# Feed-forward products of 512 moving columns where two streams, or two halves of one input, meet the same weights

## The chip, the cores and the metric

One NeuronCore of a Trainium2 chip. The metric is the device time of one launch in microseconds; three runs of the kernel before took 2554.95 us (median), 2552.15 and 2566.07 us.

## The reference

Two blocks of depth 2, all in fp32, for 256 tokens of width 1024. The first block is a mixer (convolution, attention, gated linear attention) with a feed-forward part on `x`. The second block works on two inputs, the image `x` (256 tokens) and a context (256 tokens), with the same weights for both. For each of its layers it does

- `swiglu_half_step(x, ...)` and the same on the context, with `w_ffn_up[l, 0]` and `w_ffn_down[l, 0]`;
- a modulated norm, projections, attention over both inputs and an output projection;
- `swiglu_half_step` again with the second pair of weights; in the last layer for the image alone.

`swiglu_half_step` is `x + 0.5 * mod[j+2] * ((silu(gt) * up) @ w_down)` with `gt, up = split(h @ w_up)` and `h = modulate(rms_norm(x))`; the inner width is 2816, that is 11 pairs of 256. `mod` comes from `silu(cond) @ w_ada`, for 144 weight tiles in all.

## The kernel before

**Weights.** All weights come as a stream of 510 units of 128x1024 fp32 (512 KB each). SP loads a unit into `W_raw` (`load`, L770) when the unit six places earlier is finished; ACT copies it rounded to fp32r as `W_hi` (`split`, L1448); DVE subtracts to get `W_lo` (`split`, L1825). A product of fp32 accuracy is then three fp32r products, `W_lo*x_hi`, `W_hi*x_lo` and `W_hi*x_hi` (`three`, L926 to L930). A unit is 8 weight tiles of 128x128, so it takes 24 matmuls, each with its own weight load and 256 moving columns, for one stream. PE takes unit g when `W_lo` for it is there (`weights`, L921); splits are issued three units ahead.

**Streams.** The image is stream A, the context stream B. `make_streams` lists for each the stages (norm, ffn, in2, att2, out2) and their steps; a step is a weight unit or a piece of other work. `make_order` (L305) weaves both lists by rules into one order, `ORDER`, which all engines follow: A takes a shared unit first, B takes it two or three steps later (`LAG`), and it is final when B is done. So in a feed-forward stage (66 units: 44 for up, 22 for down, in groups of six and five pairs) PE alternates 24 matmuls for A and 24 for B. PSUM is two slots of two banks for each stream (`ps`, L660), used in turn.

**Elementwise work.** After the four up units of a pair ACT takes the silu of the gate half (L1554) and DVE multiplies it with the other half out of PSUM (L2049), ACT rounds the result (L1561) and DVE takes the rest (L2055). After the down units of a group DVE adds `gate * result` to `X` (`update`, L1897; `finish_update`, L1904, for a stage's last part, which is issued in the norm of the next stage). A norm squares `X`, sums on DVE (L1917) and on PE (`norm_sums`, L1008, 1-column matmuls L1014), spreads the root on PE (L1002) and writes `H_hi` and `H_lo` (L1960).

**Conditioning.** `place_ada` (L374) gives each of 144 tiles `A_raw` a step: two DVE instructions of 1024 elements each (`ada`, L1833, L1842), loaded by SP (L778). In the second block every final unit of a feed-forward stage gets one until they are used up.

The stages that the change touches are the three joint feed-forward stages (layer 0 before and after the attention, layer 1 before it) and the image's last one, where only stream A is left.

## Time and profile before

| what | value |
|---|---|
| median of 3 runs | 2554.95 us (2552.15 to 2566.07) |
| profiled execution | span 2549.3 us; its own time is not given apart from that, and the span is 5.65 us under the median |
| PE matmul / weight load busy | 2391.4 us (94%) / 2322.8 us (91%), 20452 of each |
| DVE / ACT / POOL busy | 1661.0 us (65%) / 997.7 us (39%) / 188.2 us (7%) |
| mean granted TensorE clock | 0.966 |
| DMA | 352.78 MB, mean 138 GB/s |

A matmul's record is longer than the distance to the next one (0.28 us against about 0.12 us), since they are pipelined: the pace is read from start to start. PEld is the weight load of a matmul; a window's columns are its span, then busy us and instruction count of each engine, the granted clock of PE, the busy share of the DMA engines and GB/s.

### The profile page before, as it was taken

How to read it: one execution, taken by the hardware profiler on the slowest of the kernel's cores; microseconds unless marked ns; L12 is line 12 of the kernel's file. 1: busy time of each engine (PE TensorE's matmuls, PEld its weight loads, DVE VectorE, ACT ScalarE, POOL GpSimd, SP SyncE). 2: the span in 40 equal slices, each digit the busy share in tenths (PEclk: the TensorE clock that was granted, in tenths of full speed). 3: DMA queues.
4: the chain of work that ended last, by engine and by line, in shares of the span. 5: the costliest groups of instructions: out<-in, count | busy, mean ns of one | idle time of the engine just before them, and what ended most of it. 6: DMA issues, size and time to landing. Idle time of an engine off the chain costs nothing. (4 is left out here: it accounts for less than half of the span.)

```text
span 2549.3 us, 47682 instructions
## 1 busy us (share of the span) xinstructions
PE 2391.4 (94%) x20452; PEld 2322.8 (91%) x20452; DVE 1661.0 (65%) x2777; ACT 997.7 (39%) x1468; POOL 188.2 (7%) x300
## 2 busy tenths in 40 slices
PE   7989998899799999999788999998999998988999
PEld 7889997899799999899558999998999998967999
DVE  6789888788877777744775677776333336376554
ACT  6455664465432222322473222223222223145543
POOL 0000000370000000011000900000000000100000
PEclk9899998999899999999898999999999999999999
DMA  6246652456445555412001455552222222211454
GB/s 256 95 157 226 221 190 92 144 197 237 141 143 191 188 182 187 169 59 79 14 1 67 164 190 189 186 198 91 92 96 96 100 100 96 70 52 67 162 194 157
DMA packets 104306, 352.78 MB, mean 138 GB/s; under 512 B 18976, under 2 KB 19232, under 8 KB 103840
## 3 DMA queue, kind: packets, MB, share of 16 engines
q1 hardware_dynamic: 95904, 348.94, 38.9%
q8 instruction: 161, 2.64, 0.4%
q0 software_dynamic: 8192, 0.80, 0.3%
q14 instruction: 49, 0.40, 0.1%
HBM read 348.63 MB, written 1.05 MB: 137 GB/s over the span
## 5 line engine op out<-in xcount | busy, mean ns | idle before, releaser
L1456 ACT ACTIVATE W_hi<-W_raw 128x1024 fp32r<-128x1024 f32 x510 | 538.7, 1060 | 1119.6 <-PE slot L930 1053.9
L1830 DVE TENSOR_TENSOR W_lo<-W_raw,W_hi 128x1024 fp32r<-128x1024 f32 x510 | 621.5, 1222 | 473.8 <-ACT W_hi L1456 465.1
L928 PE MATMUL slot<-H_hiA,W_lo 128*128 128x256 f32 x2768 | 790.9, 286 | 18.0 <-DVE H_loA L1960 4.6
L929 PE MATMUL slot<-H_loA,W_hi 128*128 128x256 f32 x2768 | 781.5, 282 | 0.0
L930 PE MATMUL slot<-H_hiA,W_hi 128*128 128x256 f32 x2768 | 780.9, 282 | 0.0
L928 PEld LDWEIGHTS slot<-H_hiA,W_lo 128*128 128x128 f32 x2768 | 533.3, 193 | 29.5 <-issue 21.1
L929 PEld LDWEIGHTS slot<-H_loA,W_hi 128*128 128x128 f32 x2768 | 535.8, 194 | 0.1
L930 PEld LDWEIGHTS slot<-H_hiA,W_hi 128*128 128x128 f32 x2768 | 532.7, 192 | 0.0
L1842 DVE SCALAR_TENSOR_TENSOR PROD<-A_raw,SC 128x1024 bf16<-128x1024 f32 x288 | 341.2, 1222 | 170.3 <-DMA A_raw<-adastream 169.8
L928 PE MATMUL slot<-H_hiB,W_lo 128*128 128x256 f32 x1376 | 385.9, 280 | 3.0 <-DVE VB L2347 1.3
L929 PE MATMUL slot<-H_loB,W_hi 128*128 128x256 f32 x1376 | 383.9, 279 | 0.0
L930 PE MATMUL slot<-H_hiB,W_hi 128*128 128x256 f32 x1376 | 383.9, 279 | 0.0
L928 PE MATMUL slot<-HIDA,W_lo 128*128 128x256 f32 x1056 | 293.6, 278 | 1.2 <-DVE HIDA L2055 1.2
L929 PE MATMUL slot<-HIDA,W_hi 128*128 128x256 f32 x1056 | 293.5, 278 | 0.0
L930 PE MATMUL slot<-HIDA,W_hi 128*128 128x256 f32 x1056 | 293.5, 278 | 0.0
L928 PEld LDWEIGHTS slot<-H_hiB,W_lo 128*128 128x128 f32 x1376 | 259.2, 188 | 4.6 <-issue 2.2
L929 PEld LDWEIGHTS slot<-H_loB,W_hi 128*128 128x128 f32 x1376 | 260.7, 189 | 0.0
L930 PEld LDWEIGHTS slot<-H_hiB,W_hi 128*128 128x128 f32 x1376 | 259.7, 189 | 0.0
L928 PEld LDWEIGHTS slot<-HIDA,W_lo 128*128 128x128 f32 x1056 | 198.2, 188 | 1.6 <-DVE W_lo L1830 1.0
L929 PEld LDWEIGHTS slot<-HIDA,W_hi 128*128 128x128 f32 x1056 | 199.5, 189 | 0.0
L930 PEld LDWEIGHTS slot<-HIDA,W_hi 128*128 128x128 f32 x1056 | 198.6, 188 | 0.0
L820 POOL TENSOR_TENSOR R0A<-V_A,EXPO 128x2 f32<-128x2 f32 (+3 forms) x25 | 38.7, 1549 | 2005.2 <-DVE V_A L1868 2005.2
(277 smaller groups left out, 3057.8 us busy)
## 6 DMA issues: line engine op xcount, KB each, us to landing
W_raw<-wstream SPq DMA_DIRECT2D x510, 512.0 KB, 3.3
A_raw<-adastream SPq DMA_DIRECT2D x144, 512.0 KB, 4.3
BT<-par POOLq DMA_DIRECT2D x256, 3.0 KB, 2.6
XA<-xT SPq DMA_DIRECT2D x2, 512.0 KB, 4.5
SC<-cond SPq DMA_DIRECT2D x1, 1024.0 KB, 14.4
XB<-ctxT SPq DMA_DIRECT2D x1, 1024.0 KB, 16.4
CON<-const SPq DMA_DIRECT2D x1, 960.5 KB, 9.6
PAR<-par SPq DMA_DIRECT2D x1, 680.0 KB, 10.8
```

The costliest lines, as they stand in the source:

```text
L820: pool.tensor_tensor(s.R0[:, 0:n], s.V_[:, 0:n], EXPO[:, 0:n], ALU.pow).then_inc(s.sem.r0, 1)
L928: pe.matmul(out, wl, xh, start=start, stop=False, skip_group_check=True)
L929: pe.matmul(out, wh, xl, start=False, stop=False, skip_group_check=True)
L930: return pe.matmul(out, wh, xh, start=False, stop=stop, skip_group_check=True)
L1456: act.activation(W_hi[:, g % HIGH, :], W_raw[:, g % RAW, :], ACT.Copy).then_inc(S.w_hi, 1)
L1830: dve.tensor_tensor(W_lo[:, g % RAW, :], W_raw[:, g % RAW, :], W_hi[:, g % HIGH, :].bitcast(F32), ALU.subtract).then_inc(S.w_lo, 1)
L1842: a = dve.scalar_tensor_tensor(PROD[:, b, :], A_raw[:, slot, :], 1.0, SC[:, b, :], ALU.mult, ALU.mult, accum_out=MOD[:, t // MODS, t % MOD ...
```

## The change

Three kinds of stage take the place of `ffn` in the second block. `ffnj` (stream A) and `ffnb` (stream B) are a joint stage. Of its 66 units the first three (`LEAD`) and the last five (`TAIL`) are still done for A and for B in 24 matmuls each; the other 58 are done once, in 24 matmuls of 512 moving columns, the 256 of A and the 256 of B (`joined`). Their input tiles `HJ` and `HIDJ` are the old ones under one name, so the moving operand is two runs of 256 columns, and the result fills a PSUM bank. A unit of both streams uses four banks, half of PSUM, the halves in turn (`shared`). Silu, product, rounding and rest are one instruction for both streams. `ffns` is the image's last stage: a weight tile's `W_lo*x_hi` is a product of 256 columns, and `W_hi` meets `x_hi` and `x_lo` in one of 512, whose two results lie in two halves of a bank; ACT copies the second half out (`CORR`) and DVE adds it, or DVE adds both to `X` in turn. Its last five units are done in three products as before. The steps of `ffnb` and so the shared units are eight; the order rules are unchanged. The conditioning tiles are spread evenly over the 58 joint units of each joint stage: 48, 24 and 48 tiles in place of 62, 58 and none.

```diff
+LEAD = 3
+TAIL = GROUPS[-1][1] - GROUPS[-1][0]
...
+        if blk == 2 and not solo:
+            stages[s][-1].place = 1 if s == "A" else None
+            if s == "A":
+                st = add(s, "ffnj", steps, solo, dict(tok=PAIRS + 2 * len(GROUPS), pair=PAIRS), l=l, blk=blk, ffn=which)
+                both[l, which] = st
+                old = Old(s, 2, tok, (l, 2 * which), st.side, 0, tok)
+            else:
+                mate = both[l, which]
+                st = add(s, "ffnb", steps[:LEAD] + steps[-TAIL:], solo, dict(tok=1), l=l, blk=blk, ffn=which, mate=mate)
+                mate.mate = st
+                old = Old(s, 2, st.tok, (l, 2 * which), mate.side, 1, mate.tok + PAIRS + 2 * len(GROUPS) - 1)
+            stages[s][-1].end = old
+            side[s] = 1 - side[s]
+            return old
+        if blk == 2:
+            before = stages[s][-1]
+            side[s] = 1 - before.tok % 4 // 2
+            add(s, "ffns", steps, solo, dict(tok=PAIRS + 2 * len(GROUPS), pair=PAIRS), l=l, blk=blk, ffn=which)
+            stages[s][-1].end = Old(s, 2, tok, (l, 2 * which), side[s], 0)
+            return stages[s][-1].end
...
+    shares = {(0, 0): 2 * 3 * KT, (0, 1): 3 * KT, (1, 0): 2 * 3 * KT}
+    free = {k: [v for v in ORDER if v.stage.kind == "ffnj" and (v.stage.l, v.stage.ffn) == k and v.final] for k in shares}
+    for k, n in shares.items():
+        for i, v in enumerate(free[k]):
+            v.ada = (i + 1) * n // len(free[k]) - i * n // len(free[k])
...
-        elif st.kind == "ffn" and st.blk == 2:
-            v.ada = int(left > 4)
...
+        HJ = at("HJ", 40 * K + 192, [P, 2, 2, KT, SEQ], F32R)
+        HIDJ = at("HIDJ", AA, [P, 2, (AB - AA) // 4], F32R)
+        HFJ = at("HFJ", AA, [P, 2, (AB - AA) // 4])
...
-        slots = [ctx.enter_context(nc.psum_tensor(f"slot{i}", [P, 2, 512], F32)) for i in range(4)]
+        banks = ctx.enter_context(nc.psum_tensor("banks", [P, 8, 512], F32))
+        slots = [banks[:, 2 * i:2 * i + 2, :] for i in range(4)]
 
         def ps(st, tok):
             if st.ring == 4:
                 return slots[tok % 4]
-            return slots[tok % 2 + (2 if st.s == "B" else 0)]
+            return slots[2 * st.side + (tok % 2 if st.place is None else st.place)]
+        def shared(st, n):
+            h = 4 * ((st.side + n) % 2)
+            return banks[:, h:h + 4, :]
...
+                if st.old is not None and st.old.both is not None:
+                    pe.wait_ge(A.sem.evac, st.old.both + (s is B))
+                if st.place is not None:
+                    wait(pe, s.sem.evac, norm_token(st))
...
+            def joined(out, wl, wh, lo, hi, start, stop):
+                out = out.rearrange("p (s n) -> p s n", s=2)
+                pe.matmul(out, wl, hi, start=start, stop=False, skip_group_check=True)
+                pe.matmul(out, wh, lo, start=False, stop=False, skip_group_check=True)
+                return pe.matmul(out, wh, hi, start=False, stop=stop, skip_group_check=True)
+            def up_part(s, st, q, first):
+                wl, wh = weights()
+                p = shared(st, 0)
+                hw = s.sem.h_ready
+                h0 = (st if s is A else st.mate).hr - 8
+                for t in range(2):
+                    for k in range(4):
+                        kt = 4 * (q % 2) + k
+                        if t == 0 and q < 2:
+                            pe.wait_ge(hw, h0 + kt + 1)
+                        c = slice(256 * k + P * t, 256 * k + P * t + P)
+                        mm = three(p[:, 2 * (q // 2) + t, SEQ * s.half:SEQ * s.half + SEQ], wl[:, c], wh[:, c],
+                                   s.H_lo[:, kt, :], s.H_hi[:, kt, :], s is A and kt == 0, False)
+                mm.then_inc(s.sem.done, 1)
+            def up_both(st, n, q):
+                wl, wh = weights()
+                p = shared(st, n)
+                for t in range(2):
+                    for k in range(4):
+                        kt = 4 * (q % 2) + k
+                        c = slice(256 * k + P * t, 256 * k + P * t + P)
+                        mm = joined(p[:, 2 * (q // 2) + t, :], wl[:, c], wh[:, c], HJ[:, :, 1, kt, :],
+                                    HJ[:, :, 0, kt, :], kt == 0, kt == 7)
+                mm.then_inc(A.sem.done, 1)
+            def hidden(j, low, k):
+                o = 2 * SEQ * (2 * j + low) + SEQ * k
+                return HIDJ[:, :, o:o + SEQ]
+            def down_both(st, n, j, first, last):
+                wl, wh = weights()
+                p = shared(st, n)
+                for k in range(2):
+                    for t in range(4):
+                        c = slice(512 * k + P * t, 512 * k + P * t + P)
+                        mm = joined(p[:, t, :], wl[:, c], wh[:, c], hidden(j, 1, k), hidden(j, 0, k),
+                                    first and k == 0, last and k == 1)
+                mm.then_inc(A.sem.done, 1)
+            def down_part(s, st, old, j, first, last):
+                wl, wh = weights()
+                out = blocks(old, old.tok)
+                for k in range(2):
+                    for t in range(4):
+                        c = slice(512 * k + P * t, 512 * k + P * t + P)
+                        x = slice(SEQ * k, SEQ * k + SEQ)
+                        mm = three(out[:, t, :], wl[:, c], wh[:, c], s.HID[:, j, 1, x], s.HID[:, j, 0, x],
+                                   first and k == 0 and t % 2 == 0, last and k == 1)
+                mm.then_inc(s.sem.done, 1)
+            def doubled(bank, wl, wh, pair, start, stop):
+                pe.matmul(bank[:, 0:SEQ], wl, pair[:, 0, :], start=start, stop=False, skip_group_check=True)
+                return pe.matmul(bank.rearrange("p (s n) -> p s n", s=2), wh, pair, start=False, stop=stop,
+                                 skip_group_check=True)
+            def ffns(s, st):
+                n = 0
+                for a, b in GROUPS:
+                    for m in range(a, b):
+                        wait(pe, s.sem.evac, st.tok + n - 1)
+                        p = shared(st, n)
+                        for q in range(4):
+                            wl, wh = weights()
+                            for t in range(2):
+                                for k in range(4):
+                                    kt = 4 * (q % 2) + k
+                                    if n == 0 and t == 0 and q < 2:
+                                        pe.wait_ge(s.sem.h_ready, st.hr - 8 + kt + 1)
+                                    c = slice(256 * k + P * t, 256 * k + P * t + P)
+                                    mm = doubled(p[:, 2 * (q // 2) + t, :], wl[:, c], wh[:, c], HJ[:, s.half, :, kt, :],
+                                                 kt == 0, kt == 7)
+                            mm.then_inc(s.sem.done, 1)
+                            yield
+                        n += 1
+                    for half in range(2):
+                        pe.wait_ge(s.sem.evac, st.tok + n - 1)
+                        p = shared(st, n)
+                        for j in range(a, b):
+                            pe.wait_ge(s.sem.hid_ready, st.pair + j + 1)
+                            if b == PAIRS and half:
+                                down_part(s, st, st.end, j - a, j == a, j == b - 1)
+                                yield
+                                continue
+                            wl, wh = weights()
+                            for k in range(2):
+                                for t in range(4):
+                                    c = slice(512 * k + P * t, 512 * k + P * t + P)
+                                    x = slice(SEQ * k, SEQ * k + SEQ)
+                                    mm = doubled(p[:, t, :], wl[:, c], wh[:, c], s.HID[:, j - a, :, x],
+                                                 j == a and k == 0, j == b - 1 and k == 1)
+                            mm.then_inc(s.sem.done, 1)
+                            yield
+                        n += 1
...
+            def ffnj(s, st):
+                for q in range(LEAD):
+                    if q == 2:
+                        pe.wait_ge(A.sem.evac, st.tok)
+                    up_part(A, st, q, q == 0)
+                    yield
+                n, i = 0, LEAD
+                for a, b in GROUPS:
+                    for m in range(a, b):
+                        if n == 1:
+                            pe.wait_ge(B.sem.evac, st.mate.tok)
+                        if n:
+                            pe.wait_ge(A.sem.evac, st.tok + n - 1)
+                        for q in range(LEAD if n == 0 else 0, 4):
+                            up_both(st, n, q)
+                            i += 1
+                            yield
+                        n += 1
+                    for half in range(2):
+                        pe.wait_ge(A.sem.evac, st.tok + n - 1)
+                        for j in range(a, b):
+                            pe.wait_ge(A.sem.hid_ready, st.pair + j + 1)
+                            if i < len(st.steps) - TAIL:
+                                down_both(st, n, j - a, j == a, j == b - 1)
+                            else:
+                                down_part(A, st, st.end, j - a, j == a, j == b - 1)
+                            i += 1
+                            yield
+                        n += 1
+            def ffnb(s, st):
+                for q in range(LEAD):
+                    up_part(B, st.mate, q, False)
+                    yield
+                for j in range(TAIL):
+                    down_part(B, st, st.end, j, j == 0, j == TAIL - 1)
+                    yield
...
+            def ffns(s, st):
...
+                            if j == 0:
+                                act.wait_ge(s.sem.done, v + 4 * m + 4)
+                                wait(act, s.sem.hid_f32, pair)
+                                act.activation(CORR[:, :, :], shared(st, a + m + 2 * i)[:, :, SEQ:2 * SEQ], ACT.Copy)\
+                                   .then_inc(S.corr_out, 1)
+                                act.wait_ge(S.gate_sum, a + m + 1)
+                                act.activation(SGJ[:, 1, :], SGJ[:, 0, :], ACT.Silu).then_inc(s.sem.silued, 1)
...
+            def ffnj(s, st):
...
+                                act.activation(SGJ[:, :, :], shared(st, a + m + 2 * i)[:, 0:2, :], ACT.Silu)\
+                                   .then_inc(s.sem.silued, 1)
...
+            def update_both(st, gate, n, m, done):
+                dve.wait_ge(A.sem.done, done)
+                dve.wait_ge(A.sem.evac, st.tok + n)
+                p = shared(st, n)
+                for s in (A, B):
+                    b = p[:, :, SEQ * s.half:SEQ * s.half + SEQ]
+                    update_half(s, b, gate, m, 0)
+                    a = update_half(s, b, gate, m, 1)
+                a.then_inc(A.sem.evac, 1)
...
+            def ffns(s, st):
...
+                            if j == 0:
+                                dve.wait_ge(S.corr_out, a + m + 1)
+                                wait(dve, s.sem.silued, pair)
+                                dve.tensor_tensor(gates[:, 0, :, :], p[:, 0:2, 0:SEQ], CORR[:, 0:2, :], ALU.add)\
+                                   .then_inc(S.gate_sum, 1)
+                                step(dve.tensor_tensor(out, p[:, 2:4, 0:SEQ], CORR[:, 2:4, :], ALU.add))
+                                release(S.gate_sum, a + m + 1, s.sem.evac, st.tok + first + m)
...
+            def ffnj(s, st):
...
+                            if j == 1:
+                                dve.wait_ge(s.sem.silued, pair + 1)
+                                p = shared(st, first + m)
+                                split3 = lambda x: x.rearrange("p t (s n) -> p t s n", s=2)
+                                out = HFJ[:, :, o + 2 * SEQ:o + 4 * SEQ].rearrange("p s (t n) -> p t s n", t=2)
+                                dve.tensor_tensor(out, split3(SGJ[:, :, :]), split3(p[:, 2:4, :]), ALU.mult)\
+                                   .then_inc(s.sem.hid_f32, 1)
+                                release(s.sem.hid_f32, pair + 1, s.sem.evac, st.tok + first + m)
+                            if j == 2:
+                                dve.wait_ge(s.sem.hid_hi, pair + 1)
+                                dve.tensor_tensor(HIDJ[:, :, o + 2 * SEQ:o + 4 * SEQ], HFJ[:, :, o + 2 * SEQ:o + 4 * SEQ],
+                                                  HIDJ[:, :, o:o + 2 * SEQ].bitcast(F32), ALU.subtract)\
+                                   .then_inc(s.sem.hid_ready, 1)
...
```

## Rows read from the trace of the kernel before

**Rows 1.** The page: span, and busy time of PE and its weight loads.

```profile
span 2549.3 us, 47682 instructions
...
PE 2391.4 (94%) x20452; PEld 2322.8 (91%) x20452; DVE 1661.0 (65%) x2777; ACT 997.7 (39%) x1468; POOL 188.2 (7%) x300
```

**Rows 2.** Windows: the three joint feed-forward stages, then the image's last one.

```profile
705.00:1087.00 382.00, 373.67 (x3159) 373.23 (x3157) 276.49 (x434) 103.83 (x126) 1.39 (x2) 0.99 0.49 177
1405.00:1775.00 370.00, 363.66 (x3126) 362.94 (x3124) 263.23 (x411) 102.64 (x123) 57.20 (x120) 0.99 0.49 175
1788.00:2152.00 364.00, 355.51 (x3121) 355.08 (x3120) 130.12 (x174) 101.51 (x124) 1.40 (x2) 0.99 0.28 96
2362.00:2549.30 187.30, 182.45 (x1584) 182.12 (x1584) 101.97 (x115) 82.36 (x93) 0.00 (x0) 0.98 0.50 175
```

**Rows 3.** Windows of 50 us inside the first and the third joint stage.

```profile
750.00:800.00 50.00, 50.00 (x427) 50.00 (x426) 37.80 (x55) 14.71 (x19) 0.00 (x0) 1.00 0.51 183
1800.00:1850.00 50.00, 50.00 (x444) 50.00 (x443) 16.42 (x18) 14.31 (x18) 0.00 (x0) 1.00 0.28 96
```

**Rows 4.** Timeline of PE from 900 us, first and last of 19 (start us, us, what).

```profile
899.82 0.28 PE L928 MATMUL slot<-H_hiA,W_lo 128*128 128x256 f32 x1
...
901.94 0.28 PE L928 MATMUL slot<-HIDB,W_lo 128*128 128x256 f32 x1
```

**Rows 5.** Timeline of PE, the step at 1600 us.

```profile
1600.19 0.28 PE L930 MATMUL slot<-HIDB,W_hi 128*128 128x256 f32 x1
1600.45 0.39 PE L928 MATMUL slot<-H_hiA,W_lo 128*128 128x256 f32 x1
```

**Rows 6.** Timeline of PE from 1612 us, first and last of 20.

```profile
1611.80 0.28 PE L928 MATMUL slot<-H_hiA,W_lo 128*128 128x256 f32 x1
...
1613.95 0.28 PE L929 MATMUL slot<-H_loA,W_hi 128*128 128x256 f32 x1
```

**Rows 7.** Timeline of PE: fp32 products of 256 columns, one row for four.

```profile
123.17 1.02 PE L1275 MATMUL slot<-AC,CON 128*128 128x256 f32 x4
```

**Rows 8.** That line alone: shortest, median and longest ns.

```profile
L1275 PE MATMUL slot<-AC,CON x8: 377/378/379, 123.2 to 454.8; 128*128 128x256 f32 x8
```

**Rows 9.** Timeline of PE: 1-column products at full clock.

```profile
1068.60 1.47 PE L1014 MATMUL slot<-CON,SQA 128*128 128x1 f32 x12
```

**Rows 10.** That line alone for stream A: shortest, median, longest ns.

```profile
L1014 PE MATMUL slot<-CON,SQA x132: 164/250/353, 9.0 to 2358.0; 128*128 128x1 f32 x132
```

**Rows 11.** Timeline of PE: the same at half clock, and the first products after.

```profile
1082.01 2.69 PE L1014 MATMUL slot<-CON,SQB 128*128 128x1 f32 x12 [5.96 <-DVE SQB L1917]
1087.05 0.69 PE L1002 MATMUL slot<-CON,RSB 128*128 128x128 f32 x2 [2.35 <-DVE RSB L1874]
...
1087.75 0.42 PE L929 MATMUL slot<-H_loA,W_hi 128*128 128x256 f32 x1
1087.97 0.41 PE L930 MATMUL slot<-H_hiA,W_hi 128*128 128x256 f32 x1
```

**Rows 12.** Lines: fp32 products whose weights have 16 rows.

```profile
L1150 PE MATMUL slot<-GG,PAR x8: 374/374/478, 37.6 to 365.7; 16*128 16x256 f32 x8
```

**Rows 13.** Lines of DVE in the first joint stage (count, busy us, mean ns, idle before).

```profile
L1842 DVE SCALAR_TENSOR_TENSOR PROD<-A_raw,SC 128x1024 bf16<-128x1024 f32 x124 | 147.0, 1223 | 88.8 <-DMA A_raw<-adastream 88.5 <-DVEq L1881 0.2
L1830 DVE TENSOR_TENSOR W_lo<-W_raw,W_hi 128x1024 fp32r<-128x1024 f32 x66 | 80.6, 1220 | 13.7 <-ACT W_hi L1456 11.8 <-DVEq L1881 1.9
...
L2049 DVE TENSOR_TENSOR HFA<-SGA,slot 128x512 f32<-128x512 f32 x11 | 7.5, 683 | 0.0
...
L1892 DVE SCALAR_TENSOR_TENSOR XA<-slot,GATE,XA 128x256 f32<-128x256 f32 x16 | 6.6, 476 | 0.5 <-PE slot L930 0.5
```

**Rows 14.** Lines of ACT in the first joint stage.

```profile
L1456 ACT ACTIVATE W_hi<-W_raw 128x1024 fp32r<-128x1024 f32 x66 | 70.0, 1061 | 239.2 <-PE slot L930 239.2
...
L1554 ACT ACTIVATE SGA<-slot 128x512 f32<-128x512 f32 x11 | 6.6, 600 | 18.8 <-PE slot L930 18.8
```

**Rows 15.** Windows: where DMA moved the most.

```profile
550.00:600.00 50.00, 50.00 (x427) 50.00 (x427) 45.67 (x63) 22.71 (x25) 5.33 (x12) 1.00 0.74 259
```

145 lines of the change are left out of this document (121 added, 24 removed).

## The prediction

> **What bounds the kernel now.** I start from the page: PE is busy for 94% of the span and its weight loads for 91%, nobody else is above 65% [rows 1]. Next the windows over the stages that the change touches [rows 2]: in the three joint feed-forward stages (382, 370 and 364 us) PE is busy for 98% at a granted clock of 0.99, and in the image's last stage for 182 of 187 us. So here time is PE time, and what counts is the distance from one matmul to the next. The windows of 50 us [rows 3] show PE without any idle time in them, yet with 427 matmuls in the first stage and 444 in the third, at the same granted clock of 1.00 (2.4 GHz). The timeline gives the two paces: 18 distances between 899.82 and 901.94 us, 117.8 ns each [rows 4], and 19 between 1611.80 and 1613.95, 113.2 ns each [rows 6] (I use 113.3, of which 443 to 444 fit in 50 us). The first holds for the whole first stage and in the second up to 1600 us, where one product comes 0.26 us after its forerunner [rows 5]; afterwards the pace is the quicker one, and stays so to the end of the third stage.
>
> 256 columns alone need less. At half clock fp32r products of 256 columns follow each other in about 0.22 us [rows 11], so at full clock they would need about 107 ns. What holds them up is seen where the columns are few: 12 products of one column with a full weight load take 1.47 us, the last of them 0.25, so 111 ns each [rows 9, 10], and at half clock (2.69 - 0.35) / 11 = 213 ns [rows 10, 11]. A pair of weight load and product thus costs the load's 111 ns whatever its columns, up to about 256, and with 256 both sides are so near each other that 113.3 or 117.8 come out.
>
> **What the change does to PE.** Of the 66 units of a joint stage 58 are done in 24 products of 512 columns in place of 48 of 256. Per stage that makes 58 * 24 = 1392 pairs of products joined. Where were they? In the first stage all 1392 at 117.8 ns; in the second 33 units (36 of the first group less the three leading ones), 792 pairs, at 117.8, and 25 units, 600 pairs, at 113.3; in the third 1392 at 113.3. So 2184 pairs cost 2 * 117.8 = 235.6 ns and 1992 cost 226.6 ns.
>
> What does a product of 512 columns cost? The trace has none. Its bounds: below, twice the columns at full clock with the load wholly hidden, 213 ns (256 columns at half clock are the same number of 1.2 GHz cycles) [rows 11]; above, two old products, 226.6. The nearest row is the fp32 product of line 1275, whose four records take 1.02 us with the last 0.377 long, so 214 ns each [rows 7], and whose record is 378 ns long where that of 256 fp32r columns is 280 [rows 6, 8]; 98 ns more than the 113 to 118 of the old pace is 211 to 216. It occupies the array twice as long as an fp32r one, with a full weight load beside it, and that load doesn't show. I take 215 ns, the upper part of what these rows allow.
>
> Joint stages: 2184 * (235.6 - 215) = 45.0 us and 1992 * (226.6 - 215) = 23.1 us, together **68.1 us**.
>
> The image's last stage: 61 of its 66 units change, 8 tiles each, 488 triples. A triple was 3 * 113.3 = 340 ns. Now it is a product of 256 columns followed by one of 512. The load of the long product has to run beside the short one, so that one stays at 113.3; the other load hides. 113.3 + 215 = 328.3, so 11.7 * 488 = **5.7 us**.
>
> The Trainium skill ("TensorE: Matmul & The Clock Gate", section "Back-to-back issue gap") states a distance of N/2.4 + 2.5 ns for a warm stream; by it a pair of 256 costs 218.4, one product of 512 costs 215.8, and all that could be won in the joint stages would be about 11 us. The rows here contradict it at 256 columns.
>
> **What else changes, and what hides it.**
> - Silu, product, rounding and rest for both streams are one instruction of twice the size instead of two: ACT's 600 ns and DVE's 683 ns become about twice that at most, so no more in sum [rows 13, 14]. The result is due after a whole further pair (four units of 24 * 215 = 5.2 us), and `hid_ready` of a group's last pair is waited for four units or more after its up units.
> - `update_both` is eight times 0.41 us (16 of them are busy for 6.6 us [rows 13]) = 3.3 us in one go. It stands before the splits of two later units. Three units of weights are split ahead, 15 us; a full DVE step (1.2 for the split, 2.4 for a conditioning tile, 3.3) is 6.9 us. Hidden; without that cover 3.3 us for each of ten or so places.
> - Conditioning tiles move from the first two stages to the third. There DVE is busy for 130 of 364 us [rows 2] and gets 48 * 2.45 = 118 us more, DMA goes from 96 GB/s to under 190, which the first stage bears already. Nothing on the path; in the first stage DVE gets relief that PE doesn't feel. SP's loads of weights stand before its conditioning loads in each step, and those two queues carried the same mix before.
> - The last stage gets a copy of 1024 elements (ACT, 1.06 us by the nearest row [rows 14]) and two additions of 512 (0.68 us each [rows 13]) for a pair, four updates more for a half. In four units of 2.63 us ACT needs 4.2 + 1.1 + 0.6 + 0.6 and waits 0.7 for DVE's sum: 7.2 of 10.5 us. DVE needs 4.9 + 1.4 + 1.4. Weights are called for at 512 KB in 2.63 us, 200 GB/s; 259 were moved elsewhere [rows 15].
> - New waits on PE: A's norm waits for all earlier tokens of A. Its sums wait for squares of the same updates anyway, so the wait ends earlier than the one behind it. The wait of the third leading unit and of the second pair are for norm tokens freed when `H_lo` was done. Behind B's norm the order is the same: PE idles 5.96 us for B's squares and 2.35 us for its root at half clock before and after the change [rows 11]. B's three leading units now stand together, and the joint units wait for both; before, A had one unit in between. `H_lo` of B is complete before A's three leading units are, so nothing comes late. 0 us, at most one B unit of 2.8 us in each of three places.
>
> **Sum.** 68.1 + 5.7 = 73.8 us. The profiled span of 2549.3 becomes 2475.5; the median of the runs lies 5.65 us above the span, so 2554.95 - 73.8 = **2481 us**.
>
> **The rivals.**
> *Excess for each product.* Of the 113.3 or 117.8 ns, 6.6 or 11.1 belong to every product whatever its width. Then 512 columns cost 220 or 224.4 ns; 2184 * 11.2 + 1992 * 6.6 + 488 * 6.7 = 41 us, 2514 us. For it: two paces with no visible cause, neither of which is the load's 111. Against: line 1275 shows 214. The skill's rule above is the same mechanism with a smaller excess, and would give 2543.
> *No gain from width.* The hardware takes the two runs of 256 columns as two products, each at the old pace: 2549 to 2555 us. Against: the weight loads are halved in any case, and they set the pace.
> *The load no longer hides.* The slower side. The products of line 1150, with weights of 16 rows, have some records of 478 ns among those of 374 [rows 12]: 104 ns more, a load that stands alone. If a load waited so for the end of every long product, it would cost 320 ns in place of 231.3 (the mean of the old pairs, which is the point that decides), 4176 * 88.7 = 370 us, 2925 us. Against: with 128 rows the loads run beside their products in every row shown.
> A smaller doubt: products that stay at 256 columns run at either pace, and the gap that switches it [rows 5] may fall elsewhere. A window outside the joint stages has the slow pace too, 427 in 50 us [rows 15]; as an estimate, three such stretches, 1300 products at 4.5 ns, are 6 us either way.
>
> **How the numbers follow.** Forecast 0.77; excess for each product 0.15; no gain 0.04; load not hidden 0.04. The range: below, 213 instead of 215 ns (9 us) and 6 us of pace, 2466; above, up to the second case, 2515. That leaves out 8% of rivals and the edges of the first two. Half a per cent (12.8 us) is about what a measurement of this kernel can tell from no change. Both leading cases are faster by more: 0.92; within 0.5% 0.04; slower 0.04.
>
> **What would show it.** In the profile after: matmuls of 128x512 with starts 215 ns apart, in stretches of either old pace; 58 units of about 5.2 us, joint stages of some 353, 347 and 348 us; matmuls fewer by 4176 + 488; in the last stage triples of 328 ns. The paces of the 256-column products next to them tell whether the switch moved. Wrong it would be by distances of 220 or more, by PE idle before `W_lo` or `HIDJ`, or by a longer wait for B's squares than 5.96 us.

## The result, and the profile after

The changed kernel takes **2578.80 us** (median of 9 runs, 2572.84 to 2583.67) against 2555.91 us (9 runs, 2545.60 to 2573.63) of the kernel before: ratio 1.0095, 95% interval 1.0064 to 1.0125. It is slower by about 1%, where 2481 us was forecast. The profiled executions have spans of 2571.0 and 2549.3 us, so 21.7 us are to be explained. Runs more than 1.5% above the fastest of their kernel stand in the ranges given here, but not in the ratios.

The page of the changed kernel, the lines that answer to [rows 1], and one of its groups of matmuls:

```profile
span 2571.0 us, 38123 instructions
PE 2411.0 (94%) x15788; PEld 2129.8 (83%) x15788; DVE 1674.2 (65%) x2745; ACT 996.1 (39%) x1413; POOL 188.4 (7%) x300
L1130 PE MATMUL banks<-HJ,W_hi 128*128 128x512 f32 x984 | 389.2, 396 | 0.0
```

The matmuls are fewer by 20452 - 15788 = 4664 = 4176 + 488, so the change does all that it says. Weight loads were busy for 91% of the span and are now for 83%: they have been relieved, and PE has not become quicker. A product of 512 columns has a record of 396 ns, where the fp32 product from which I had priced it has 378 [rows 8]. Windows of 50 us in the first and the third joint stage (as [rows 3]) and in the image's last stage:

```profile
750.00:800.00 50.00, 50.00 (x216) 40.30 (x215) 33.16 (x45) 14.19 (x14) 0.00 (x0) 1.00 0.50 169
1800.00:1850.00 50.00, 50.00 (x216) 40.26 (x215) 30.33 (x38) 12.88 (x14) 0.00 (x0) 1.00 0.44 148
2400.00:2450.00 50.00, 50.00 (x285) 43.42 (x284) 31.39 (x35) 27.78 (x31) 0.00 (x0) 1.00 0.60 184
```

PE has no idle time and the clock is granted in full, as before. But 216 products of 512 fit where 427 or 444 of 256 did. A window also counts the one or two products that overlap its edges, so the distance is taken from the timeline of PE, between the first and last start of a stretch. Here 26 distances in the first joint stage, and then nine triples of the last stage:

```profile
899.77 0.40 PE L1130 MATMUL banks<-HIDJ,W_hi 128*128 128x512 f32 x1
900.01 0.39 PE L1131 MATMUL banks<-HIDJ,W_hi 128*128 128x512 f32 x1
900.24 0.40 PE L1129 MATMUL banks<-HIDJ,W_lo 128*128 128x512 f32 x1
...
905.84 0.40 PE L1129 MATMUL banks<-HIDJ,W_lo 128*128 128x512 f32 x1
```

```profile
2399.76 0.28 PE L1190 MATMUL banks<-HJ,W_lo 128*128 128x256 f32 x1
2399.88 0.40 PE L1191 MATMUL banks<-HJ,W_hi 128*128 128x512 f32 x1
2400.12 0.28 PE L1190 MATMUL banks<-HJ,W_lo 128*128 128x256 f32 x1
...
2402.95 0.28 PE L1190 MATMUL banks<-HJ,W_lo 128*128 128x256 f32 x1
```

(905.84 - 899.77) / 26 = 233.5 ns; over many such stretches it is **233.3 ns**, in all three joint stages, whatever the pace of the products of 256 around them. It is a mean of two values: in the trace's nanoseconds 236.0 and 230.7 take turns (213 distances from 750 to 800 us), and as they go by twos and the products of a weight tile by threes, each of the three products has one value and then the other. A triple costs (2402.95 - 2399.76) / 9 = 354 ns (353.3 over more of them), the short product 118 of it and the long one 235. Forecast were 215 and 328.3.

Did a wait come in? The sums of the squares in front of each norm are landmarks that both kernels have. The timeline of PE of the changed kernel has them here, five times B's and then A's of the last stage, from the second on with the idle time before it:

```profile
692.85 0.35 PE L1064 MATMUL banks<-CON,SQB 128*128 128x1 f32 x1
1081.97 0.34 PE L1064 MATMUL banks<-CON,SQB 128*128 128x1 f32 x1 [6.04 <-DVE SQB L2169]
1391.67 0.34 PE L1064 MATMUL banks<-CON,SQB 128*128 128x1 f32 x1 [7.53 <-DVE SQB L2169]
1775.00 0.34 PE L1064 MATMUL banks<-CON,SQB 128*128 128x1 f32 x1 [5.96 <-DVE SQB L2169]
2159.38 0.34 PE L1064 MATMUL banks<-CON,SQB 128*128 128x1 f32 x1 [6.04 <-DVE SQB L2169]
2370.48 0.34 PE L1064 MATMUL banks<-CON,SQA 128*128 128x1 f32 x1 [4.13 <-DVE SQA L2169]
```

and the kernel before has the first and the last four of them here:

```profile
688.82 0.35 PE L1014 MATMUL slot<-CON,SQB 128*128 128x1 f32 x1
1389.97 0.34 PE L1014 MATMUL slot<-CON,SQB 128*128 128x1 f32 x1 [7.60 <-DVE SQB L1917]
1772.58 0.34 PE L1014 MATMUL slot<-CON,SQB 128*128 128x1 f32 x1 [5.96 <-DVE SQB L1917]
2146.70 0.34 PE L1014 MATMUL slot<-CON,SQB 128*128 128x1 f32 x1 [5.96 <-DVE SQB L1917]
2355.68 0.34 PE L1014 MATMUL slot<-CON,SQA 128*128 128x1 f32 x1 [4.24 <-DVE SQA L1917]
```

The idle times are the old ones within 0.1 us (the one left out stands in [rows 11] with 5.96 at 1082.01). The differences of the landmarks give the time by stage: +4.0 us in front of the first joint stage, -0.04 at its end, +1.7 after the attention behind it, +2.4 after the second joint stage, **+12.7 after the third**, +14.8 at the start of the last stage, **+21.7** at the end. So within the stages that the change touches the loss lies in the third joint stage (10.3 us) and in the last one (6.9 us), and these are the stretches in which the kernel before had its quick pace. The distances account for it: 2184 pairs that had cost 235.6 ns cost 2.3 ns less, -5 us; 1992 pairs that had cost 226.6 cost 6.7 more, +13.3 us; 488 triples cost 353.3 instead of 340, +6.5 us. That makes 14.8 us. By stage it is -3.2, +2.2 and +9.3 for the joint stages, where the landmarks give -4.1, +0.7 and +10.3. The other 7.9 us lie outside these stages: 4.0 before the first joint one (692.85 against 688.82 us) and 3.9 in the two attention parts, where nothing is joined. In the first of these stretches it is the clock: PE has half clock for 78 us of it, where the kernel before has 65 (the mean over the whole execution is 0.961 and was 0.966). As an estimate, those 13 us more cost up to 6.5 us, and 613 fewer distances at 117.8 ns give 2.7 back, so up to 3.8 of the 4.0 us. In the third joint stage 3.4 us more at half clock are up to 1.7 us.

**Theory W (width):** an fp32r column has its own price, above 1/2.4 ns, whatever the width; the weight load was never the limit. **Rivals:** L, the weight load still sets the distance; R, the jump between the two runs of 256 in the moving operand does; K, consecutive writes to one bank do; P, each product has 20 ns on top of its columns, whatever its width. (The expectations call W theory C or B, and K theory S.) The question beside them is why 256 columns cost 113.3 at one time and 117.8 at another.

### The profile page after: what moved, and what is told of

It is laid out like the page before. It is cut to its first block and busy times, and to the rows that moved or that the text cites. A ratio compares the mean times of both kernels' runs of the same rounds, so it can differ in the third digit from the quotient of the medians.

```text
span 2571.0 us, 38123 instructions
## 1 busy us (share of the span) xinstructions
PE 2411.0 (94%) x15788; PEld 2129.8 (83%) x15788; DVE 1674.2 (65%) x2745; ACT 996.1 (39%) x1413; POOL 188.4 (7%) x300
## 5 line engine op out<-in xcount | busy, mean ns | idle before, releaser
L974 PE MATMUL banks<-HJ,W_lo 128*128 128x256 f32 x1824 | 528.7, 290 | 19.2 <-DVE HJ L2209 4.4
L975 PE MATMUL banks<-HJ,W_hi 128*128 128x256 f32 x1824 | 518.3, 284 | 0.0
L976 PE MATMUL banks<-HJ,W_hi 128*128 128x256 f32 x1824 | 517.7, 284 | 0.0
L1130 PE MATMUL banks<-HJ,W_hi 128*128 128x512 f32 x984 | 389.2, 396 | 0.0
L1131 PE MATMUL banks<-HJ,W_hi 128*128 128x512 f32 x984 | 389.2, 396 | 0.0
L1129 PE MATMUL banks<-HJ,W_lo 128*128 128x512 f32 x984 | 389.2, 395 | 0.0
L974 PEld LDWEIGHTS banks<-HJ,W_lo 128*128 128x128 f32 x1824 | 356.2, 195 | 30.9 <-issue 20.7
L975 PEld LDWEIGHTS banks<-HJ,W_hi 128*128 128x128 f32 x1824 | 355.9, 195 | 0.1
L976 PEld LDWEIGHTS banks<-HJ,W_hi 128*128 128x128 f32 x1824 | 354.8, 195 | 0.0
L1131 PEld LDWEIGHTS banks<-HJ,W_hi 128*128 128x128 f32 x984 | 185.0, 188 | 44.6
L1129 PEld LDWEIGHTS banks<-HJ,W_lo 128*128 128x128 f32 x984 | 185.0, 188 | 44.5
L1130 PEld LDWEIGHTS banks<-HJ,W_hi 128*128 128x128 f32 x984 | 185.0, 188 | 44.4
L974 PE MATMUL banks<-HIDJ,W_lo 128*128 128x256 f32 x632 | 176.3, 279 | 1.8 <-DVE HIDJ L2307 1.7
L975 PE MATMUL banks<-HIDJ,W_hi 128*128 128x256 f32 x632 | 175.4, 278 | 0.0
L976 PE MATMUL banks<-HIDJ,W_hi 128*128 128x256 f32 x632 | 175.4, 278 | 0.0
L1129 PE MATMUL banks<-HIDJ,W_lo 128*128 128x512 f32 x408 | 161.4, 396 | 0.0
L1130 PE MATMUL banks<-HIDJ,W_hi 128*128 128x512 f32 x408 | 161.4, 396 | 0.0
L1131 PE MATMUL banks<-HIDJ,W_hi 128*128 128x512 f32 x408 | 161.4, 396 | 0.0
```

The costliest lines, as they stand in the source:

```text
L974: pe.matmul(out, wl, xh, start=start, stop=False, skip_group_check=True)
L975: pe.matmul(out, wh, xl, start=False, stop=False, skip_group_check=True)
L976: return pe.matmul(out, wh, xh, start=False, stop=stop, skip_group_check=True)
L1129: pe.matmul(out, wl, hi, start=start, stop=False, skip_group_check=True)
L1130: pe.matmul(out, wh, lo, start=False, stop=False, skip_group_check=True)
L1131: return pe.matmul(out, wh, hi, start=False, stop=stop, skip_group_check=True)
```

## Experiments

The probes p1, p2, p5, p7 and p8 change only what the joint products multiply, each of the three joint stages in its own way (stages 0-0, 0-1 and 1-0 of the code). What they compute there is another thing than the reference; the order of instructions, waits and loads is that of the changed kernel. Their total times therefore say nothing, their distances do. All edits are shown shortened. Expectations call the kernels' stages "first", "second" and "third".

### p1: one run, 384 columns, narrow weights

```diff
+ if key == (0, 0): hi, lo = one_run[0], one_run[1]      # 512 columns in one run of HJ
+ if key == (0, 1): out, hi, lo = out[:, :, 0:192], hi[:, :, 0:192], lo[:, :, 0:192]
+ if key == (1, 0): out, wl, wh = out[0:64], wl[:, 0:64], wh[:, 0:64]
```

> Three probes in one kernel, one for each joint stage; results are not the reference's. First stage: the moving operand of every 512-column product is one run of 512 columns (two neighbouring tiles of stream A) in place of two runs of 256. Second stage: 2 runs of 192, so 384 columns. Third stage: 512 columns, but weights of 64 columns, so half a load and 64 output rows. Theory R (the switch between two runs costs the time): first stage 215 ns a product, second 160 + 18 = 178, third 233. Theory C (at full clock fp32r columns enter at 233.3 / 512 = 0.456 ns each): 233, 175, 233. Theory L (the weight load beside the product takes turns from it): 233, 180, 223. Theory P (an excess of 20 ns for each product whatever its size): 233, 180, 233; at 384 columns C and P are 5 ns apart.

Measured, by windows inside the three stages:

```profile
850.00:900.00 50.00, 50.00 (x216) 40.30 (x215) 33.34 (x54) 10.50 (x10) 0.00 (x0) 1.00 0.48 169
1450.00:1500.00 50.00, 50.00 (x290) 50.00 (x290) 32.96 (x39) 18.41 (x19) 8.85 (x19) 1.00 0.55 180
1850.00:1900.00 50.00, 50.00 (x216) 29.07 (x215) 32.48 (x54) 9.55 (x9) 0.00 (x0) 1.00 0.49 168
```

One run of 512 columns is as slow as two (216; start to start 233.3 ns), which ends R. With weights of 64 columns the loads are busy for 29.07 us in place of 40.30 and the products come 0.6 ns sooner (216; 232.7 ns), which ends L for 512 columns. 384 columns cost 173.3 ns (36 distances in 6.24 us), 13.3 above 384/2.4, where P had 180.

### p2: bf16, two banks in turn, 320 columns

```diff
+ if key == (0, 0): wl = wh = HALF[:, 0:P]; hi = lo = HALF[:, P:P + 512]   # bf16 ones
+ if key == (0, 1): outs = [pair[n], pair[1 - n], pair[n]]                 # banks in turn
+ if key == (1, 0): outs, hi, lo = [out[:, :, 0:160]] * 3, hi[:, :, 0:160], lo[:, :, 0:160]
```

> Three probes in one kernel; results are not the reference's. First stage: both operands of the 512-column products are bf16 (one constant tile, 512 columns in one run). Second stage: consecutive products write to different PSUM banks in turn. Third stage: 2 runs of 160, so 320 columns. Theory C with bytes as its reason (fp32r operands come in slower than the array takes them at full clock): 213 to 216 ns, 233, 146. Theory S (adding to the bank that was just written costs it): 233 (fp32 results are added there too), 213 to 216, 146 to 153. Theory R (two runs): 215, 233, 133 + 18 = 151. Theory P (fixed excess of 20 ns): 233, 233, 153.

The timeline of PE in the first stage, first and last of 15, and the window of the second:

```profile
900.80 0.38 PE L1143 MATMUL banks<-HALF 128*128 128x512 bf16 x1
...
903.82 0.38 PE L1142 MATMUL banks<-HALF 128*128 128x512 bf16 x1
1450.00:1500.00 50.00, 50.00 (x216) 40.30 (x215) 23.25 (x27) 13.47 (x14) 0.00 (x0) 1.00 0.41 135
```

bf16 needs 3.02 / 14 = 215.7 ns. The Trainium skill ("TensorE: Matmul & The Clock Gate", "Back-to-back issue gap") has N/2.4 + 2.5 ns, 215.8 for 512: this probe agrees with it, so the rule that I had set aside holds, here for bf16 only. The section calls it the gap of an isolated product, and gives about 131 ns for 512 columns in a stream of loads and products; no run here shows that. Two banks in turn change nothing (216; 233.3 ns), which ends K. 320 columns take 146.7 ns (42 distances in 6.16 us), as W expected.

### p5: constants in fp32r, 448 and 480 columns

```diff
+ if key == (0, 0): wl = wh = CONST[:, 0:P]; hi = lo = CONST[:, P:P + 512]   # fp32r ones, one run
+ if key == (0, 1): out, hi, lo = out[:, :, 0:224], hi[:, :, 0:224], lo[:, :, 0:224]
+ if key == (1, 0): out, hi, lo = out[:, :, 0:240], hi[:, :, 0:240], lo[:, :, 0:240]
```

> Three probes in one kernel; results are not the reference's. So far 256 columns cost 6.7 or 11.1 ns over their columns at 2.4 GHz, 320 and 384 cost 13.3, 512 cost 20.0, and 512 bf16 columns 2.3. First stage: the control to the bf16 probe, both operands fp32r from one constant tile of ones, 512 columns in one run. Second stage: 2 runs of 224, 448 columns; third: 2 runs of 240, 480 columns. Theory B (four-byte columns are what cannot come in at 2.4 GHz without stalls, whatever they hold): 233 ns; and stalls of 6.7 ns, one more for every 170 to 190 columns: 448 columns 186.7 + 13.3 to 20 = 200 to 207, 480 columns 220. Theory A (the address changes or the data, not the width of a column, cost it): the constant tile gives 216.

The timeline of the first stage, first and last of 28, then the windows of the second and third:

```profile
899.78 0.39 PE L1140 MATMUL banks<-CONST 128*128 128x512 f32 x1
...
905.90 0.39 PE L1140 MATMUL banks<-CONST 128*128 128x512 f32 x1
1500.00:1550.00 50.00, 50.00 (x249) 46.31 (x248) 28.26 (x40) 13.27 (x13) 0.00 (x0) 1.00 0.44 148
1900.00:1950.00 50.00, 50.00 (x236) 44.07 (x235) 35.71 (x52) 11.46 (x12) 0.00 (x0) 1.00 0.54 188
```

With constants 512 fp32r columns take 6.12 / 27 = 226.7 ns, that is 2 * 113.3: **a column costs in the quick pace of the kernel before what it costs in a product of 512 from constants**, 0.443 ns. Neither 233 nor 216, the two expectations, came out. 448 columns take 202.7, 480 take 213.3 where 220 was expected. All widths together, with the excess over N/2.4:

| columns | 256 | 320 | 384 | 448 | 480 | 512 | 512, constants | 512, bf16 |
|---|---|---|---|---|---|---|---|---|
| ns | 113.3 / 117.8 | 146.7 | 173.3 | 202.7 | 213.3 | 233.3 | 226.7 | 215.7 |
| excess | 6.7 / 11.1 | 13.3 | 13.3 | 16.0 | 13.3 | 20.0 | 13.3 | 2.4 |

No width between is cheaper per column than 256 at its quick pace.

### p7: which of the two operands

```diff
+ if key == (0, 0): wl = wh = CONST[:, 0:P]              # constant weights, real moving columns
+ if key == (0, 1): hi = lo = CONST[:, P:P + 512]        # real weights, constant moving columns
+ if key == (1, 0):                                      # bf16: upper halves, every second element
+     wl = wh = HALF[:, :]; hi, lo = (x.bitcast(BF16)[:, :, 1:2 * SEQ:2] for x in (hi, lo))
```

> Three probes in one kernel, 512 columns each; results are not the reference's. fp32r operands out of one constant tile had cost 226.7 ns, real ones 233.3, bf16 ones 215.7. First stage: constant weights with the real moving operand. Second stage: constant moving operand (one run) with the real weights. Third stage: bf16 throughout, a constant weight tile, and as moving operand the upper halves of the real tiles, so every second bf16 value: two bytes a column but four bytes of stride. If the excess belongs to the moving columns, the first stage stays at 233 and the second shows 227; if to the weight load beside it, the reverse. If the memory delivers lines of bytes, the stride costs as much as fp32r and the third stage shows 226 to 233; if the width of the element in the array decides, 216.

```profile
850.00:900.00 50.00, 50.00 (x220) 41.00 (x220) 34.07 (x54) 11.42 (x12) 0.00 (x0) 1.00 0.53 181
1600.00:1650.00 50.00, 50.00 (x217) 40.55 (x216) 23.30 (x31) 11.21 (x12) 0.00 (x0) 1.00 0.41 137
1950.00:2000.00 50.00, 50.00 (x222) 21.20 (x221) 35.44 (x60) 9.53 (x9) 0.00 (x0) 1.00 0.54 187
```

By the timeline 228.9, 232.3 and 226.7 ns. The third is the telling one: elements of bf16 that stand **four bytes apart** cost 226.7, like fp32r with constants, not 215.7. So it is the spacing of the moving columns in memory, not the arithmetic. The first two share out the last 6.7 ns: 4.4 of them go when the weights come from the constant tile, 1.0 when the moving columns do, and I can't say why. The values are an unlikely reason, since in the changed kernel the same product comes at 236.0 and at 230.7 ns in turn.

### p8: spacing of the columns

```diff
+ if key[0] == 0: wl, wh = (x.bitcast(BF16)[:, 1:2 * P:2] for x in (wl, wh))
+ if key == (0, 0): hi = lo = HALF[:, :]                                          # 2 bytes apart
+ if key == (0, 1): hi, lo = (x.bitcast(BF16)[:, :, 1:2 * SEQ:2] for x in (hi, lo))  # 4 bytes
+ if key == (1, 0): hi, lo = spaced                      # fp32r, every second column: 8 bytes
```

> Three probes in one kernel, 512 columns each; results are not the reference's. So far: bf16 without gaps 215.7 ns, bf16 values four bytes apart with a constant weight tile 226.7, fp32r with a constant weight tile 228.9, fp32r with real weights 233.3. First stage: bf16 columns without gaps from a constant tile, weights the upper halves of the real ones (four bytes apart). Second stage: upper halves for both operands, so the addresses of the real kernel with elements of two bytes. Third stage: fp32r columns eight bytes apart. Theory M (the stream of addresses into the memory is what counts, element width doesn't): about 216, 233, and well over 233 for the third. Theory E (the four-byte element in the array counts): 216, 226 or less, 233. If the real weights' load alone disturbs the stream, the first shows 222.

```profile
800.00:850.00 50.00, 50.00 (x233) 22.63 (x232) 36.22 (x47) 13.84 (x14) 0.00 (x0) 1.00 0.55 193
1600.00:1650.00 50.00, 50.00 (x222) 21.43 (x221) 24.61 (x29) 13.24 (x13) 0.00 (x0) 1.00 0.41 137
2000.00:2050.00 50.00, 50.00 (x111) 22.86 (x111) 17.73 (x23) 5.40 (x6) 0.00 (x0) 1.00 0.27 95
```

By the timeline 215.8 ns with columns 2 bytes apart (and real weights), 226.7 with 4, 453.3 with 8 (110 distances), which is twice 226.7. From 4 bytes on the pace of a long product is a pace of bytes passed over; 2 bytes save only 5%. The expectation of 233 for real data in the second stage missed: the upper halves of both real operands, as bf16, take 226.7. In the third stage both operands are real and fp32r, and nothing is left above twice 226.7, so real data alone don't bring the last 6.7 ns either. The Trainium skill ("SBUF — State Buffer", "Door 1: The DMA port swizzle") tells of lines of 16 bytes in which fp32 can be strided up to 4 elements without loss; this probe has 4 bytes against 8 bytes at double the time, so for the moving operand the measurement decides against it.

### p6: a cut product as a switch of the pace

The kernel before, with one product in every fourth unit of A cut in two, another cut in each of the four stages shown (joint stages 128+128, 64+192, 240+16, last stage 32+224).

```diff
+ pe.matmul(out[:, 0:cut], wl, xh[:, 0:cut], start=start, stop=False, skip_group_check=True)
+ pe.matmul(out[:, cut:], wl, xh[:, cut:], start=False, stop=False, skip_group_check=True)
```

> The kernel before, with one product in every fourth unit of stream A cut in two of the same weights: 128 + 128 columns in the first joint stage, 64 + 192 in the second, 240 + 16 in the third, 32 + 224 in the image's last one; nothing is left out. The two paces of products of 256 columns (113.3 and 117.8 ns) are the question. Theory F (the pace is a state of the stream that a product of another width resets, in the same way each time): inside a stage the pace after a cut is always the same one, and one width that leads to 113.3 would win 4.4 ns a product. Theory Z (it is set once, at a stage's start or by something outside PE): the pace doesn't answer to the cuts, and they cost 100 ns each.

```profile
750.00:800.00 50.00, 50.00 (x442) 49.95 (x441) 37.15 (x54) 14.55 (x18) 0.00 (x0) 1.00 0.56 195
1450.00:1500.00 50.00, 50.00 (x443) 50.00 (x443) 37.94 (x58) 14.63 (x18) 11.62 (x25) 1.00 0.57 199
1800.00:1850.00 50.00, 50.00 (x437) 50.00 (x436) 16.26 (x18) 14.27 (x18) 0.00 (x0) 1.00 0.28 95
```

The first two stages ran quickly from beginning to end, where [rows 3] had 427 in the first; that a cut brought this isn't shown. The third began slowly and went to 113.3 at its third cut, the last stage at its second; nowhere did a cut turn quick into slow. The pace is thus a state that a short product can change, and only sometimes. Both theories fell: F, by which a form of cut acts in one way each time, and Z, by which the pace doesn't answer to cuts. Its time, 2557.08 us in one run, is within the spread of the kernel before.

### e1 and e2: each part of the change alone

e1 keeps the joint products, and the last stage is the old one; e2 has the new last stage and the old joint ones. In e2_last_only B's second half is added to the stream from A's accumulators, so that its data, not its work, are other ones; e2b_last_only reads B's own. Both have the conditioning placed as in the kernel before.

```diff
- if blk == 2:                 # e1: the pairing of the last stage off
+ if blk == 2 and False:
- if blk == 2 and not solo:    # e2, e2b: the joint products off
+ if blk == 2 and not solo and False:
```

> The changed kernel with the image's last stage as it was before (three products of 256 columns). Joint stages as in the changed kernel: 4176 products at 233.3 ns. If the parts simply add, the last stage is back at 113.3 or 117.8 ns a product: 6.5 us less than the changed kernel or the same, so 2572 to 2579 us beside a kernel before of 2556.

> The kernel before with the new last stage of the image alone (one product of 256 and one of 512 columns for a weight tile). Triples of 353.3 ns in place of 340 at the quick pace or 353.3 at the slow one: 0 to 6.5 us over the kernel before, so 2556 to 2562 us. If more than that is lost, the copy and the additions of that stage are on the path.

> As the run with the new last stage of the image alone, but with stream B's updates read from its own accumulators (there they came from A's). The time should be the same within the scatter, 2556 to 2562 us, and the last stage's triples 353.3 ns again.

| kernel | us, median (range, runs) | ratio to before, 95% |
|---|---|---|
| e1_joint_only | 2574.59 (2567.84 to 2580.47, 10) | 1.0074 [1.0038, 1.0109] |
| e2_last_only | 2556.25 (2549.40 to 2574.93, 10) | 0.9993 [0.9959, 1.0027] |
| e2b_last_only | 2554.57 (2539.24 to 2573.51, 12) | 1.0021 [0.9985, 1.0058] |

Windows of e1's first joint stage and of e2b's last stage:

```profile
750.00:800.00 50.00, 50.00 (x216) 40.27 (x215) 32.45 (x42) 13.28 (x13) 0.00 (x0) 1.00 0.49 176
```

```profile
2400.00:2450.00 50.00, 50.00 (x285) 43.42 (x285) 31.80 (x39) 24.73 (x28) 0.00 (x0) 1.00 0.56 189
```

e1 came out as expected (2572 to 2579 us): the joint products carry most of the loss. The last stage alone can't be told from no change. Its distances are the same 353.3 as in the full change, which is 6.5 us, or 0.25%, against a stage at the quick pace, and the interval holds both that and nothing. Against a last stage at the slow pace, 3 * 117.8 = 353.4 ns a triple, it would cost nothing; no trace shows such a stage from end to end, p6 shows the first 12 us of one.

### e3 and e4: the pace held, before and after

If short products lead to the quick pace, cuts of 240+16 at the places where stages begin should hold the kernel before there. e3 is the kernel before with 48 cut products (the first of A's units 4 to 8 and 36 to 38 in each of its six feed-forward stages); e4 is the changed kernel with the 16 of them that lie in the first block, whose stages the change leaves alone.

```diff
+ CUT_AT = (4, 5, 6, 7, 8, 36, 37, 38)
+ if v.stage.kind == "ffn" and v.s == "A" and v.i in CUT_AT and now.cut != (v.stage, v.i):
+     pe.matmul(out[:, 0:240], wl, xh[:, 0:240], start=start, stop=False, skip_group_check=True)
+     pe.matmul(out[:, 240:], wl, xh[:, 240:], start=False, stop=False, skip_group_check=True)
```

> The kernel before with 48 products cut into 240 + 16 columns (in each feed-forward stage the first product of units 4 to 8 and 36 to 38 of stream A); nothing is left out. Theory F (products of 256 columns run in one of two states, 113.3 or 117.8 ns, and a short product brings the slow one to the quick one and never back): every feed-forward stage is at 113.3 from unit 8 on. The profiled execution of the kernel before had some 6100 of its feed-forward products in the slow state, 27 us; the cuts cost 48 * 0.115 = 5.5 us; 2530 to 2545 us beside 2556, and a narrower spread of the runs. Theory Z (the state is not PE's, it comes and goes by itself): 2562 us and the spread as before.

> The changed kernel with the same cut products (240 + 16 columns, units 4 to 8 and 36 to 38) in the first block's two feed-forward stages; in the joint stages these units are joined and stay as they are; nothing is left out. If the kernel before really lives on its pace, and the cuts hold it at 113.3 ns, then the change against the kernel before with cuts (2536 us) costs 4176 * 6.7 + 488 * 13.3 = 34 us less 32 cuts saved (3.7 us): 2566 us, and 10 us under the changed kernel without cuts. If the joint products' pace is worth no more than the 22 us seen, the two stay 22 us apart: 2558 us.

| kernel | us, median (range, runs) | ratio to before, 95% |
|---|---|---|
| before, beside e3 | 2557.69 (2530.52 to 2579.91, 23) | |
| e3_cuts_before | **2536.18** (2529.43 to 2545.09, 12) | **0.9938 [0.9909, 0.9968]** |
| before, beside e4 | 2557.41 (2535.54 to 2576.74, 17) | |
| e4_changed_with_cuts | 2565.48 (2558.86 to 2577.61, 12) | 1.0039 [1.0014, 1.0065] |

Windows of e3, and then those of e4 in the same joint stages:

```profile
200.00:250.00 50.00, 50.00 (x426) 50.00 (x426) 43.33 (x67) 29.55 (x39) 0.00 (x0) 1.00 0.61 203
600.00:650.00 50.00, 50.00 (x442) 50.00 (x442) 42.33 (x64) 31.08 (x42) 0.00 (x0) 1.00 0.64 216
750.00:800.00 50.00, 50.00 (x444) 50.00 (x443) 38.48 (x57) 15.29 (x19) 0.00 (x0) 1.00 0.55 191
1800.00:1850.00 50.00, 50.00 (x443) 50.00 (x443) 16.42 (x18) 14.39 (x18) 0.00 (x0) 1.00 0.29 96
```

```profile
750.00:800.00 50.00, 50.00 (x216) 40.30 (x215) 32.27 (x42) 13.28 (x13) 0.00 (x0) 1.00 0.48 166
1800.00:1850.00 50.00, 50.00 (x215) 40.25 (x215) 31.78 (x41) 14.19 (x14) 0.00 (x0) 1.00 0.46 158
```

The timeline of PE in e3 shows a cut that changed the pace. Before these rows 47 products stand 117.8 ns apart, after them 47 at 113.7:

```profile
1591.00 0.27 PE L933 MATMUL slot<-H_hiA,W_lo 128*128 128x240 f32 x1
1591.11 0.18 PE L934 MATMUL slot<-H_hiA,W_lo 128*128 128x16 f32 x1
1591.14 0.36 PE L937 MATMUL slot<-H_loA,W_hi 128*128 128x256 f32 x1
1591.34 0.28 PE L938 MATMUL slot<-H_hiA,W_hi 128*128 128x256 f32 x1
```

and here it is lost: before the stall 22 products 113.8 ns apart, after the cut that follows it at once, 117.7 for 10 us and more, up to the cuts near 600 us.

```profile
518.72 0.28 PE L938 MATMUL slot<-H_hiA,W_hi 128*128 128x256 f32 x1
520.30 0.35 PE L933 MATMUL slot<-H_hiA,W_lo 128*128 128x240 f32 x1 [1.31 <-DVE W_lo L1838]
```

e3 **beats both kernels**, by 0.6% against the kernel before, as expected (2530 to 2545 us), and its runs lie within 16 us where those of before spread over 49 (36 for the 19 of them in the ratio). The clock doesn't explain it: the mean over the runs is 0.9647 against 0.9639, which as an estimate is 2 us. The hold isn't perfect. The same wait for `W_lo` at the start of the first stage lost the quick pace too (the window with 426), and near 265, 600 and 1585 us a cut changed nothing before the next one did. Nor does this one execution show where the gain of the runs comes from. Its first joint stage has 444 products in 50 us where [rows 3] had 427, but it was at 113.3 ns before its first cut, and so were the three stages after it. The cuts that changed the pace are those at 268, 603 and 1591 us. The first joint stage can be quick without any cut, as in e2_last_only:

```profile
750.00:800.00 50.00, 50.00 (x443) 50.00 (x443) 37.68 (x57) 15.00 (x19) 0.00 (x0) 1.00 0.58 192
```

e4 came out as expected (2566 us). With the cuts on both sides the change costs 2565.48 - 2536.18 = 29.3 us, a difference between two sets of runs whose kernels before agree within 0.3 us. The same by distances, 4176 * 6.7 + 488 * 13.3 = 34.5 us, less e3's 32 further cuts at 0.11 us, 3.5: 31.

## Why the prediction was wrong

**Joint stages**, forecast -68.1 us: by the distances -5 + 13.3 = +8.3 us. The split of the 4176 pairs over the two paces was right for that execution (in e2_last_only the old first stage is quick), and it decides the sign: joined products gain 2.3 ns on a slow pair and lose 6.7 on a quick one. **Last stage**, forecast -5.7 us: +6.5 by the distances (353.3 instead of 328.3 a triple). "That one stays at 113.3" was off by 5, the 215 ns of the long one by 20.

**What was to be hidden was hidden.** The new instructions twice as wide (HIDJ 1219 ns on DVE, SGJ 1008 on ACT), the conditioning moved to the third joint stage (DVE busy for 240 of 374 us there, 130 before [rows 2]), the new order around the norms: the windows have no PE idle, and the waits for B's squares behind the three joint stages are 6.04, 5.96 and 6.04 us, where each had been 5.96. "0 us" for these waits stands.

**The rivals.** "Excess for each product" had the right kind of mechanism and, with 224.4 ns at most, half the size: the excess isn't one sum a product, it grows from 6.7 to 13.3 as the columns double and then has 6.7 on top. "No gain from width" (226.7 or 235.6) was nearest, and its reason, two products in one, was not the cause. "The load no longer hides" is refuted: no product came 320 ns after its forerunner, and p1's narrower loads gain 0.6 ns. None of the cases held the outcome, slower at 233.3 ns, because I gave the distance of a long product a ceiling that no row showed. The Trainium skill's rule (215.8) was, for this dtype, as wrong as my figure.

## What to carry to other kernels

Take the price of a product from rows of its own dtype and of its own spacing in memory, start to start: 214 ns for a pass of fp32 said nothing of 512 columns of fp32r. Where a number stands near another, change one of them alone before calling it the cause, above all when the whole gain hangs on it. If a PE-bound kernel of fp32r products of 256 columns varies by 1 to 2% from run to run, count the products in equal windows: there may be two paces, and a cheap cut can hold the better one.

## What was not expected of the hardware

- **The moving operand has a price by spacing.** 512 columns 2, 4 and 8 bytes apart: 215.8, 226.7 and 453.3 ns at the full clock. Four bytes means 17/16 of 512/2.4, and for 256 columns 113.3 is the same 17/16 of 106.7; real data of 320 to 480 columns lie 0.8 to 5.0 ns above that.
- **Operands from a constant tile cost less than the kernel's own.** At 512 columns fp32r: constants in both operands 226.7 ns, constant weights 228.9, constant moving operand 232.3, real in both 233.3. The cause stays open: the constants are one tile at one place, used again and again, and neither the values themselves nor the place nor the reuse was varied alone. The turns of 236.0 and 230.7 ns and p8's 453.3 speak against the values. 230.7 is near 113.3 + 117.8 and 236.0 near 2 * 117.8, so it may be the same thing as the two paces. With the granted clock at 1.00 in all of them it isn't the clock.
- **Two paces at one clock.** 256 columns come 113.3 or 117.8 ns apart for hundreds of us, and the state changes at stalls [rows 5] or short products (e3, p6). The kernel before has 17,184 such products in lines 928 to 930; its spread of 49 us (2530.52 to 2579.91) is what 11,000 of them at 4.5 ns would make. That e3's spread is a third of it speaks for that cause; that its median is 21.5 us lower is shown. The clock has a part in it too: it lay between 0.961 and 0.968 in the runs beside e3, by estimate up to 18 us. What in the chip holds the state, and why one cut in several changes it, stays open, and whether cuts behind the waits for `W_lo` would bring e3 lower wasn't tried.
